# A two-layer encoder kernel: where the squares of its norms are added

## What is computed

```python
def rms_norm(x, g):
    y = x * rsqrt(mean(x * x, axis=-1, keepdims=True) + 1e-6)
    return y * g

for l in range(2):
    g = norm_g[l]
    x = x + 0.5 * rms_norm(swiglu(rms_norm(x, g[0]), ...), g[1])
    x = x + rms_norm(mixer(rms_norm(x, g[2]), ...), g[3])   # even: Fourier + conv, odd: short conv
    x = x + rms_norm(cross_attention(rms_norm(x, g[4]), rms_norm(mem, mem_g[l]), ...), g[5])
    x = x + 0.5 * rms_norm(swiglu(rms_norm(x, g[6]), ...), g[7])
```

## Time and profile before

| | |
|---|---|
| runs, us | 3093.03, 3094.83, 3095.97; median 3094.83 |
| profiled execution | span 3095.2 us on core 4, the slowest; cores 3083.2 to 3095.2 |
| mean granted TensorE clock | 0.962 on core 4, 0.962 to 0.967 over the cores |
| PE busy | 2887.6 us, 93%, 12868 matmul records |
| DVE busy | 997.3 us, 32% |
| ACT busy | 1058.7 us, 34% |
| POOL busy | 616.3 us, 20% |
| matmuls on squares of X (sqp) | x251 records, 449 ns each, 65.7 us of PE idle ahead of them |
| PE's share of the chain that ended last | 82% |

### The profile page before, as it was taken

The page is one execution under the profiler, slowest core; times in us unless marked ns, Lnnn a source line. Parts: engine busy times, 40 slices in busy tenths (PEclk is TensorE's granted clock), DMA queues, the critical chain, the costliest instruction groups (busy, mean ns, idle before and its releaser), DMA issues.

```text
span 3095.2 us, 37991 instructions; the slowest of 8 cores (3083.2 to 3095.2 us)
## 1 busy us (share of the span) xinstructions
PE 2887.6 (93%) x12868; PEld 1289.7 (42%) x13124; DVE 997.3 (32%) x1429; ACT 1058.7 (34%) x1588; POOL 616.3 (20%) x930
## 2 busy tenths in 40 slices
PE   6999999889888889999999999996998898999997
PEld 2444444333333434444444444442443443444443
DVE  2212312242236346205105105105544427312312
ACT  4113313214764564124124124122115376213112
POOL 1114113110022122114112114112003204111111
PEclk9999999889988999999999999997999998999998
DMA  7544544352023434544544444541233522444667
GB/s 168 76 67 77 79 68 81 53 81 37 14 47 50 71 52 67 75 73 74 77 70 78 75 69 79 77 70 28 41 59 48 93 41 47 73 72 85 124 90 144
DMA packets 122715, 220.47 MB, mean 71 GB/s; under 512 B 12704, under 2 KB 24224, under 8 KB 122528
## 3 DMA queue, kind: packets, MB, share of 16 engines
q0 software_dynamic: 111920, 198.99, 41.4%
q1 hardware_dynamic: 10608, 19.03, 1.9%
HBM read 408.52 MB, written 8.39 MB: 135 GB/s over the span
## 4 chain that ended last, share of the span: by engine, by line
PE 82%; DVE 7%; ACT 6%; issue 3%; DMA 2%; POOL 0%; DVEq 0%; ACTq 0%; SPq 0%; POOLq 0%
PE ps L220 82%; DVE HO L618 2%; DVE XN L529 1%; DVE HO_103 L618 1%; DVE X L620 1%; DMA slot_47<-wflat 1%; ACT sqp L523 1%; DVE DG_77 L795 0%; DVE DG_78 L795 0%; DMA slot_45<-wflat 0%; ACT L937 0%; ACT sqp L516 0%; DMA X<-xT 0%; ACT L461 0%; DVE H L746 0%
## 5 line engine op out<-in xcount | busy, mean ns | idle before, releaser
L746 DVE TENSOR_TENSOR H<-ps,s_58 128x512 bf16<-128x512 f32 x176 | 121.4, 690 | 751.1 <-PE ps L220 742.7
L575 ACT ACTIVATE HO<-ps,cf_sb 128x512 f32<-128x512 f32 x224 | 154.0, 687 | 522.3 <-PE ps L220 499.6
L220 PE MATMUL ps<-XN,slot_44 128*128 128x512 bf16 x892 | 243.9, 402 | 45.5 <-DVE XN L529 40.6
L737 ACT ACTIVATE s_58<-ps 128x512 f32<-128x512 f32 x176 | 105.2, 598 | 417.6 <-PE ps L220 377.2
L746 DVE TENSOR_TENSOR H<-ps,s_59 128x512 bf16<-128x512 f32 x176 | 121.5, 690 | 365.0 <-PE ps L220 348.9
L737 ACT ACTIVATE s_59<-ps 128x512 f32<-128x512 f32 x176 | 105.0, 597 | 383.7 <-PE ps L220 354.8
L220 PE MATMUL ps<-XN,slot_45 128*128 128x512 bf16 x897 | 223.7, 394 | 0.7
L220 PE MATMUL ps<-XN,slot_49 128*128 128x512 bf16 x894 | 216.2, 383 | 1.0
L220 PE MATMUL ps<-XN,slot_46 128*128 128x512 bf16 x896 | 212.5, 379 | 1.6 <-DVE H L746 0.9
L220 PE MATMUL ps<-XN,slot_51 128*128 128x512 bf16 x890 | 212.8, 379 | 1.2
L220 PE MATMUL ps<-XN,slot_47 128*128 128x512 bf16 x895 | 213.0, 379 | 0.9
(11 more groups left out here) (300 smaller groups left out, 4078.4 us busy)
## 6 DMA issues: line engine op xcount, KB each, us to landing
slot_44<-wflat POOLq DMA_DIRECT2D x88, 256.0 KB, 3.8
slot_45<-wflat POOLq DMA_DIRECT2D x88, 256.0 KB, 4.7
slot_46<-wflat POOLq DMA_DIRECT2D x88, 256.0 KB, 4.0
slot_47<-wflat POOLq DMA_DIRECT2D x88, 256.0 KB, 4.8
slot_48<-wflat POOLq DMA_DIRECT2D x88, 256.0 KB, 4.1
slot_49<-wflat POOLq DMA_DIRECT2D x88, 256.0 KB, 5.0
slot_50<-wflat POOLq DMA_DIRECT2D x88, 256.0 KB, 3.9
slot_51<-wflat POOLq DMA_DIRECT2D x88, 256.0 KB, 4.9
```

The source lines that it names most:

```text
L220: fn = (lambda e, l_=l_, r_=r_, st=st, sp=sp: e.matmul(out, lhsT=l_, rhs=r_, start=st, stop=sp))
L575: k.op("act", lambda e: e.activation(out=oap, in_=P[bank][:, :], func=AF.Copy, scale=gcol), reads=[("P", bank)] + CONST, writes=okeys)
L737: k.op("act", lambda e, bg=bg, s=s: e.activation(out=SS[s][:, :], in_=P[bg][:, :], func=AF.Silu), reads=[("P", bg)], writes=[("S", s)])
L746: k.op("dve", lambda e, bu=bu, s=s, hap=hap: e.tensor_tensor(out=hap, in0=P[bu][:, :], in1=SS[s][:, :], op=ALU.mult), reads=[("P", bu), (" ...
```

## The change

The sums over chunks go from PE to DVE. In the post-norm, ACT's Square of chunk 0 is written in float32 into the place of the block's HO chunk 7 (`acc`); for chunks 1 to 6 the Square goes to sqd, of which there are now two, and DVE adds it to acc; for chunk 7 DVE adds into a bfloat16 tile sqf, and only then is HO chunk 7 itself written. `stat_mm` has one matmul per block in place of eight. In the pre-norm DVE reduces the four chunks of sqp to one tile sb (which shares its space with the silu's buffers s), and one matmul takes the place of four; it happens twice per block.

```diff
-    SQD = [sb("sqd%d" % i, OFF_SQ + i * 1024, [TB], BF16) for i in range(3)]
+    SQD = [sb("sqd%d" % i, OFF_SQ + i * 1024, [TB], BF16) for i in range(2)]
+    SQF = [sb("sqf%d" % i, OFF_SQ + (2 + i) * 1024, [TB], BF16) for i in range(2)]
...
+    SB = [sb("sb%d" % i, OFF_S + i * 2048, [TB], BF16) for i in range(2)]
...
+            def sq_sum(first):
+                s = k.rot("S", 2)
+
+                def red(e):
+                    with nc.allow_low_precision(reason="summed in float32, rounded once for the matmul"):
+                        return e.tensor_reduce(out=SB[s][:, :], in_=SQP[:, :, :].rearrange("p c t -> p t c"),
+                                               op=ALU.add, axis=AX.X)
+                k.op("dve", red,
+                     reads=[("SQP",)], writes=[("S", s)])
+                k.mm(P[st["b"]][:, :], [(ONESM[:, :], SB[s][:, :], [("S", s), ("ONES",)])], st["b"], start=first, stop=not first)
+
             def sb_():
-                st["b"] = bnk = k.bank(reserve=True)
-                for c in range(4):
-                    k.mm(P[bnk][:, :], [(ONESM[:, :], SQP[:, c, :], [("SQP",), ("ONES",)])], bnk, start=(c == 0), stop=False)
+                st["b"] = k.bank(reserve=True)
+                sq_sum(True)
...
-                for c in range(4):
-                    k.mm(P[bnk][:, :], [(ONESM[:, :], SQP[:, c, :], [("SQP",), ("ONES",)])], bnk, start=False, stop=(c == 3))
+                sq_sum(False)
...
+                acc, acck = self.hoap(7, tl)
+
+                def scaled():
+                    k.op("act", lambda e: e.activation(out=oap, in_=P[bank][:, :], func=AF.Copy, scale=gcol),
+                         reads=[("P", bank)] + CONST, writes=okeys)
+                if c == 0:
+                    scaled()
+                    k.op("act", lambda e: e.activation(out=acc, in_=P[bank][:, :], func=AF.Square),
+                         reads=[("P", bank)], writes=acck)
+                    return
+                i = k.rot("SQD", 2)
                 k.op("act", lambda e: e.activation(out=SQD[i][:, :], in_=P[bank][:, :], func=AF.Square),
                      reads=[("P", bank)], writes=[("SQD", i)])
-                self.pend.append((tb, c, i))
-                self.stat_mm(2)
+                if c < 7:
+                    k.op("dve", lambda e: e.tensor_tensor(out=acc, in0=acc, in1=SQD[i][:, :], op=ALU.add),
+                         reads=acck + [("SQD", i)], writes=acck)
+                    scaled()
+                    return
+                f = tb % 2
+                k.op("dve", lambda e: e.tensor_tensor(out=SQF[f][:, :], in0=acc, in1=SQD[i][:, :], op=ALU.add),
+                     reads=acck + [("SQD", i)], writes=[("SQF", f)])
+                scaled()
+                self.pend.append((tb, f))
```

More of the change, by code:

```diff
@@ L9 @@
 ALU = mybir.AluOpType
+AX = mybir.AxisListType
 D = 1024
@@ L30 @@
 OFF_SQ = OFF_SLOTS + NSLOT * 2048
-OFF_R = OFF_SQ + 7 * 1024
+OFF_R = OFF_SQ + 8 * 1024
 OFF_S = OFF_R + 2 * 2048
@@ L39 @@
 OFF_ONES = OFF_CB + NCB * 2
-OFF_END = OFF_ONES + 256 + 256 + 512
+OFF_END = OFF_ONES + 256 + 256
 assert SB_BASE + OFF_END <= SB_TOP, (SB_BASE + OFF_END, SB_TOP)
@@ L390, in build @@
     SLOTS = [sb("slot%d" % i, OFF_SLOTS + i * 2048, [SLOT_ELEMS], BF16) for i in range(NSLOT)]
-    SQD = [sb("sqd%d" % i, OFF_SQ + i * 1024, [TB], BF16) for i in range(3)]
-    SQP = sb("sqp", OFF_SQ + 3 * 1024, [4, TB], BF16)
+    SQD = [sb("sqd%d" % i, OFF_SQ + i * 1024, [TB], BF16) for i in range(2)]
+    SQF = [sb("sqf%d" % i, OFF_SQ + (2 + i) * 1024, [TB], BF16) for i in range(2)]
+    SQP = sb("sqp", OFF_SQ + 4 * 1024, [4, TB], BF16)
     R = [sb("r%d" % i, OFF_R + i * 2048, [TB], F32) for i in range(2)]
     SS = [sb("s%d" % i, OFF_S + i * 2048, [TB], F32) for i in range(2)]
+    SB = [sb("sb%d" % i, OFF_S + i * 2048, [TB], BF16) for i in range(2)]
     CF = sb("cf_sb", OFF_CF, [NCF], F32)
@@ L398, in build @@
     ONES1 = sb("ones1", OFF_ONES + 256, [128], BF16)
-    ONESF = sb("onesf", OFF_ONES + 512, [128], F32)
     P = [nc.alloc_psum_tensor("ps%d" % i, [128, TB], F32) for i in range(8)]
@@ L455, in program @@
         k.op("dve", lambda e: e.memset(ONES1[:, :], 1.0), writes=[("ONES",)])
-        k.op("dve", lambda e: e.memset(ONESF[:, :], 1.0 / 128.0), writes=[("ONES",)])
         CONST = [("CF",), ("CB",), ("ONES",)]
@@ L574, in evac @@
                 gcol = G(self.l, self.n, c)
-                k.op("act", lambda e: e.activation(out=oap, in_=P[bank][:, :], func=AF.Copy, scale=gcol),
-                     reads=[("P", bank)] + CONST, writes=okeys)
-                i = k.rot("SQD", 3)
+                acc, acck = self.hoap(7, tl)
[8 more added lines that the diff above has]
+                i = k.rot("SQD", 2)
                 k.op("act", lambda e: e.activation(out=SQD[i][:, :], in_=P[bank][:, :], func=AF.Square),
                      reads=[("P", bank)], writes=[("SQD", i)])
-                self.pend.append((tb, c, i))
-                self.stat_mm(2)
+                if c < 7:
[8 more added lines that the diff above has]
+                self.pend.append((tb, f))
             def stat_mm(self, keep):
@@ L586, in stat_mm @@
                 while len(self.pend) > keep:
[L587 to L592, removed]
+                    tb, f = self.pend.pop(0)
+                    self.pst[tb] = bnk = k.bank(reserve=True)
+                    k.mm(P[bnk][:, :], [(ONESM[:, :], SQF[f][:, :], [("SQF", f), ("ONES",)])], bnk)
             def finish(self, nxt, hf, cpb=1):
-                fin_stats = keyed(lambda: self.stat_mm(0), [("SQD", i_) for i_ in range(3)], [])
+                fin_stats = keyed(lambda: self.stat_mm(0), [("SQF", i_) for i_ in range(2)], [])
                 ta, tb_ = self.tbs[0], self.tbs[-1]
```

## The result

| | before | changed |
|---|---|---|
| runs, us | 3093.03, 3094.83, 3095.97 | 3387.88, 3389.22, 3390.28 |
| median of the three, us | 3094.83 | 3389.22 |
| ratio | 1 | 1.0951, 95% interval 1.0932 to 1.0969 |
| profiled execution, span | 3095.2 (core 4) | 3388.7 (core 6) |
| mean granted TensorE clock | 0.962 | 0.916 |

The forecast was 3241 with a range of 3110 to 3285. The direction held, and the loss of 294 us is twice the 146 of the sum.

A forecast was written before the change was run, and what follows sets the result against it. The kernel was taken as PE-bound in plain stages, with PE waiting on ACT and DVE chains between sublayers. Losses of 143.6 and 24, less 22, plus 0.5, gave +146 on 3094.83: 3241 us, range 3110 to 3285.

The forecast's parts named there:

- I take 2.35: Pre-norm: each DVE reduction of four chunks was taken to last 2.35 us, like the two-input pass over 128x2048.
- Rival 4: Pre-norm reductions read with a 1 KB step and run at half speed, 4.7 us each: 3356 us; chance 8%.
- Each 0.1 us moves the sum by 4.9: Whole kernel: each 0.1 us of a reduction's duration was said to move the summed change by about 4.9 us.
- the start: Start of the program: the first reductions cost what their matmuls saved, 0.
- the dense stages: Pre-norms inside dense FFN stages: PE stands still for each reduction; +6.2 us at each of four places, +24.
- behind attention: Stretch after attention: new reductions stand in DVE's queue and PE's gate and up matmuls wait behind them; +13 us each.
- FFN down: FFN down projections: the adds hide in idle DVE and 112 matmuls go; a gain of 22 us.
- the mixers' matmuls held up by HO chunk 7: Mixers, output projection's second half: ACT waits for chunk 7, so matmuls end at 936.5 instead of 921.9, +14.6 us each.
- attention held up by two square buffers and the adds: Attention, second half: ACT stops at the third square until DVE's adds begin, and PE waits for banks; +15 us each.
- the third reduction behind eight products: Pre-norms after a mixer's projection: the second block's first reduction queues behind eight DVE products, about 2 us more.
- ACT held at chunk 0: Mixers, second half: ACT's first Square waits until all eight chunks are added to X, 18 us after its present start.
- Rival 5: Post-norm adds on DVE slow down beside POOL, 14 adds at +0.7 costing 10 us a transition: 3280 us; chance 4%.

The follow-up runs named there:

- e8_forms: The kernel before with nine DVE forms added at its very end, to time each; four values side by side took 2.286 us, two chunks 1.220 us.
- e11_tiny_op: The changed kernel with a copy of 4 columns in place of each reduction, three of four chunks left out of the sum; 3175.6 us.

## Why the prediction was wrong

The direction, the post-norm's half and the list of places were right, and the size of the pre-norm's half was not: 119 us forecast, 255 measured.

- *The reduction.* The step that failed first is "I take 2.35". The bounds from the nearest rows, 1.29 to 2.76, did not hold the 3.60, and by e8_forms the reason is the access pattern: every one of those rows reads its operands side by side. Rival 4 named the stride and had the sign right, at 8%. Its 3356 lies nearest to the measured time, but by luck: it had 4.7 us a reduction, and with 3.6 its sum would have been 3302. At 0.98 us per us and 64 places the 1.25 us cost 78 of the missing 148.
- *Each 0.1 us moves the sum by 4.9.* It moves it by 6.3: next to nothing of a reduction is hidden anywhere. At 2.35 that is 32 us.
- *The places.* With reductions of next to no length my terms would have come to about +31; e11_tiny_op, less the 14 us of its own copies, is at about +66. The rest of the miss is here, some 35. By the ledger, at equal duration (and so with the 32 of the point before in it), it lies at the start (0 in the sum, 21 measured, 11 of it not by the longer reduction), in the dense stages (24 against 70, 26 of it so) and behind attention (26 against 53, 17 of it so). In the dense stages the waits were right and the term that was put at nothing is PE's lower clock behind each wait, some 28 us.
- *Right:* FFN down (-22 against -22.9), the mixers' matmuls held up by HO chunk 7 (+18.1 against +18.9), attention held up by two square buffers and the adds (19.0 us of ACT's wait), the third reduction behind eight products. ACT held at chunk 0 for 20.2 us was put at 18. Rival 5 did not come up: the adds took 0.69 us, but none of the 224 ran beside an instruction of POOL, so what one costs there isn't shown.
- *Wrong in the range:* 3110 to 3285 took its upper end from a duration that I had bounded by rows of another access pattern. For an operation and an access pattern that the trace doesn't show I should have taken a wider upper end times the count of places at which PE waits for it.

## What to carry to other kernels

A matmul that reads an operand straight from the engine that made it cost 0.22 us in a dense stage here; to save three of them by one instruction on a third engine puts that engine's whole queue in front of PE. Count hand-overs before you count matmuls: here each cost 1.3 us at next to no work, plus the full length of the work. The same sum on DVE was worth 3.0 us a stage where DVE was idle and nobody waited for the parts, so split such a change by stage and keep those.

## What the hardware showed unexpectedly

- A reduction of four values 1 KB apart took 3.59 us for 2048 elements, of four side by side 2.29, and of two values 1 KB apart 1.22 for 1024 elements, as fast per element as side by side. In float32, 4 KB apart, it was 3.62.
- ACT's Square of 128x2048 took 1.91 us with its output in order and 4.79 us with a step of 8 bytes.
- In a dense stage a wait of 4.8 us was followed by 24 matmuls in 8.07 us, in place of 5.3, with a granted clock of 0.50 for the first 3.6 us.
